# The 32x32 diagonal blocks of a triangular inverse: TensorE doubling levels, or substitution on GpSimd

## The reference

```
decay = exp(where(incl, g[..., :, None] - g[..., None, :], NEG_INF))
L = where(strict, einsum('bhnid,bhnjd->bhnij', kb, k) * decay, 0.0)
T = triangular_solve(L + eye, eye, left_side=True, lower=True)
u = einsum('bhnij,bhnje->bhnie', T, vb)
```

## Time and profile before

| What | Value |
|---|---|
| Median of 3 runs | 1326.43 us (1325.88 to 1328.53) |
| Span of the profiled execution | 1324.9 us; the page gives no other time of that execution |
| TensorE busy | 1280.8 us, 97% of the span |
| VectorE busy | 797.9 us, 60% |
| ScalarE busy | 614.3 us, 46% |
| GpSimd busy | 22.8 us, 2% |
| Mean granted TensorE clock | 0.990 of full speed |
| HBM read | 219.22 MB, 169 GB/s over the span with the writes |

### The profile page before, as it was taken

The page is one execution under the profiler, slowest core; times in us unless marked ns, Lnnn a source line. Parts: engine busy times, 40 slices in busy tenths (PEclk is TensorE's granted clock), DMA queues, the critical chain, the costliest instruction groups (busy, mean ns, idle before and its releaser), DMA issues. The chain is left out here.

```text
span 1324.9 us, 17917 instructions
## 1 busy us (share of the span) xinstructions
PE 1280.8 (97%) x7296; PEld 1110.6 (84%) x7296; DVE 797.9 (60%) x1064; ACT 614.3 (46%) x869; POOL 22.8 (2%) x36
## 2 busy tenths in 40 slices
PE   7999999999999999999999999799999999999996
PEld 6999988998998878888888888678888787878885
DVE  5668776764775455546454555567466766466553
ACT  4555545223422445543444444254445555466443
POOL 0100000000000000000000000000000000000000
PEclk9999999999999999999999999899999999999998
DMA  8646554444444454566666686455645654454662
GB/s 276 181 128 193 177 184 131 128 128 134 127 138 130 128 176 140 174 189 191 189 193 187 193 318 197 128 190 162 188 143 159 192 159 143 143 192 155 223 193 79
DMA packets 119778, 224.58 MB, mean 170 GB/s; under 512 B 9409, under 2 KB 20833, under 8 KB 118545
## 3 DMA queue, kind: packets, MB, share of 16 engines
q1 hardware_dynamic: 118386, 213.81, 52.9%
q0 software_dynamic: 1312, 9.63, 2.0%
HBM read 219.22 MB, written 4.19 MB: 169 GB/s over the span
## 5 line engine op out<-in xcount | busy, mean ns | idle before, releaser
L1076 DVE TENSOR_TENSOR lo_w<-raw_w,hi_w 128x1024 fp32r<-128x1024 f32 x396 | 479.5, 1221 | 337.2 <-ACT hi_w L740 336.3
L740 ACT ACTIVATE hi_w<-raw_w 128x1024 fp32r<-128x1024 f32 x396 | 410.2, 1055 | 287.5 <-PE acc L1645 202.7
L1645 PE MATMUL acc<-hi_w,h_hi 128*128 128x512 f32 (+1 forms) x832 | 333.3, 401 | 2.9 <-DVE h_lo L1084 2.6
L1645 PE MATMUL acc<-hi_w,h_lo 128*128 128x512 f32 (+1 forms) x832 | 322.8, 388 | 0.0
L1645 PE MATMUL acc<-lo_w,h_hi 128*128 128x512 f32 (+1 forms) x832 | 321.9, 387 | 0.0
L1645 PEld LDWEIGHTS acc<-hi_w,h_hi 128*128 128x128 f32 x832 | 157.5, 189 | 34.3 <-issue 5.0
L1636 PE MATMUL acc<-h_hi,hi_w 128*128 128x256 f32 x640 | 184.4, 288 | 1.4 <-DVE lo_w L1076 1.4
L1645 PEld LDWEIGHTS acc<-hi_w,h_lo 128*128 128x128 f32 x832 | 157.0, 189 | 33.1
L1645 PEld LDWEIGHTS acc<-lo_w,h_hi 128*128 128x128 f32 x832 | 157.6, 189 | 29.7 <-issue 0.7
L1636 PE MATMUL acc<-h_hi,lo_w 128*128 128x256 f32 x640 | 181.0, 283 | 0.0
L1636 PE MATMUL acc<-h_lo,hi_w 128*128 128x256 f32 x640 | 180.9, 283 | 0.0
(11 more groups left out here) (319 smaller groups left out, 1262.0 us busy)
## 6 DMA issues: line engine op xcount, KB each, us to landing
raw_w<-in_w_in SPq DMA_DIRECT2D x284, 512.0 KB, 3.8
raw_w<-in_w_out SPq DMA_DIRECT2D x64, 512.0 KB, 4.7
raw_w<-in_w_branch_a SPq DMA_DIRECT2D x16, 512.0 KB, 4.5
raw_w<-in_w_branch_b SPq DMA_DIRECT2D x16, 512.0 KB, 4.7
raw_w<-in_cmp_k_w SPq DMA_DIRECT2D x8, 512.0 KB, 4.3
raw_w<-in_cmp_v_w SPq DMA_DIRECT2D x8, 512.0 KB, 4.1
x_in<-in_x SPq DMA_DIRECT2D x4, 512.0 KB, 6.0
x<-in_x POOLq DMA_DIRECT2D x1, 2048.0 KB, 10.5
```

Source lines behind the costliest of these rows:

```text
L740: act.activation(hi_w[slot][:, 0:n], raw_w[no % RAW_SLOTS][:, 0:n], ACT.Copy).then_inc(*hi_ready.event(no))
L1076: dve.tensor_tensor(lo_w[slot][:, 0:n], raw_w[no % RAW_SLOTS][:, 0:n], hi_w[slot][:, 0:n].bitcast(F32), ALU.subtract).then_inc(*lo_ready.e ...
L1645: i = pe.matmul(to[:, t, 0:group.cols], x[at], w[:, k], start=first and k == 0 and m == 0, stop=last and k == n - 1 and m == 2)
```

## The change

The diagonal blocks of 32x32 of all 16 matrices (4 blocks each, 64 blocks) are no longer built by levels 2 to 5. As soon as a chain's `tri` is done, GpSimd issues four DMAs (`blocks_away`), one for each row of blocks, that write them to DRAM. When all are there, `solve` loads the 64 blocks, one to a partition with 1024 values, sets the diagonal to one, and inverts each by substitution: 31 steps of an outer product and an addition, with a wait after each instruction. It writes the result to DRAM, and eight DMAs (32 partitions, 8 heads, runs of 128 bytes) put it on the diagonal of `inv_t`, which was zeroed at the start. `lift` (VectorE) keeps the upper triangle and prepares level 6; levels 6 and 7 stay. The plan puts the first parts of all four chains in ticks 55 to 72, the solve at 73, the lifts at ticks 91, 94, 99 and 102, both quads' recurrence by tick 112. `low_t` gets a buffer for each chain, and quad 1's `gu` waits for the outgoing blocks of quad 0, whose tile it overwrites.

The plan, and the new or changed steps:

```diff
+            s = base + 4 * (NT * h + t)
             at(s, "gu", h, t)
             at(s + 1, "gram", h, t)
             at(s + 2, "decay", h, t)
             at(s + 3, "tri", h, t)
             at(s + 4, "tri_flip", h, t)
-            at(s + 5, "invert_first", h, t)
-            for n in range(2, LEVELS + 1):
-                at(s + 8 + 3 * (n - 2), "invert_y", h, t, n)
-                at(s + 9 + 3 * (n - 2), "invert_t", h, t, n)
+            at(s + 5, "blocks_away", h, t)
+    at(base + 18, "solve")
+    base += 36
+    for h in range(2):
+        for t in range(NT):
+            s = base + 8 * h + 3 * t
+            at(s, "lift", h, t)
+            for n in range(BLOCK_LEVELS + 1, LEVELS + 1):
+                at(s + 1 + 3 * (n - BLOCK_LEVELS - 1), "invert_y", h, t, n)
+                at(s + 2 + 3 * (n - BLOCK_LEVELS - 1), "invert_t", h, t, n)
                 if n < LEVELS:
-                    at(s + 10 + 3 * (n - 2), "invert_flip", h, t, n)
-        s = base + 29
+                    at(s + 3 + 3 * (n - BLOCK_LEVELS - 1), "invert_flip", h, t, n)
+        s = base + 8 * h + 9
         for n in range(5):
             at(s + n, "delta", h, n)
...
+            pool.memset(inv_t[:], 0.0).then_inc(*pool_did.event("inv_zero"))
...
+            def blocks_away(h, t):
+                pool.wait_ge(*dve_did.after("tri", h, t))
+                for b in range(4):
+                    pool.dma_start(block_scratch[0][b, t, quad(h)].rearrange("i r c -> r i c"),
+                                   diagonal_block(chain[t]["wide"], b)).then_inc(*blocks_out[h][t].event(b))
+
+            def solve():
+                for h in range(2):
+                    for t in range(NT):
+                        pool.wait_ge(*blocks_out[h][t].after(3))
+                x = small_block
+                n = x.shape[0]
+                pool.dma_start(x[:], block_scratch[0].rearrange("b t i r c -> (b t i) r c")).then_inc(
+                    *blocks_in.event(0))
+                pool.wait_ge(*blocks_in.after(0))
+                link(pool.memset(x[:].rearrange("p r c -> p (r c)")[:, 0:BLOCK * BLOCK:BLOCK + 1], 1.0))
+                for j in range(BLOCK - 1):
+                    rows, cols = j + 1, BLOCK - 1 - j
+                    term = small_term[:, 0:rows * cols].rearrange("p (r c) -> p r c", c=cols)
+                    link(pool.tensor_tensor(term, x[:, j + 1:BLOCK, j].unsqueeze(1).broadcast_to([n, rows, cols]),
+                                            x[:, 0:rows, j].unsqueeze(2).broadcast_to([n, rows, cols]), ALU.mult))
+                    to = x[:, 0:rows, j + 1:BLOCK]
+                    last = pool.tensor_tensor(to, to, term, ALU.add)
+                    if j < BLOCK - 2:
+                        link(last)
+                last.then_inc(*pool_did.event("solved"))
+                pool.wait_ge(*pool_did.after("solved"))
+                pool.dma_start(block_scratch[1].rearrange("b t i r c -> (b t i) r c"), x[:]).then_inc(
+                    *solved_out.event(0))
+                pool.wait_ge(*solved_out.after(0))
+                for b in range(4):
+                    for t in range(NT):
+                        pool.dma_start(diagonal_block(inv_t[:, :, t], b),
+                                       block_scratch[1][b, t].rearrange("i r c -> r i c")).then_inc(
+                            *blocks_back.event(b, t))
...
+                if h:
+                    dve.wait_ge(*blocks_out[0][t].after(3))
+                    dve.wait_ge(*act_did.after("tri_flip", 0, t))
                 dve.tensor_tensor(chain[t]["wide"][:], over_heads(upto[:]), over_cols(g[:, o:o + QUAD]),
                                   ALU.mult).then_inc(*dve_did.event("gu", h, t))
...
+            def lift(h, t):
+
                 inv_q = inv_t[:, quad(h), t]
-                dve.wait_ge(*act_did.after("tri_flip", h, t))
-                dve.tensor_tensor(c["inv"][:], c["wide"][:], over_heads(levels[:, 1]), ALU.mult)
-                link(dve.tensor_tensor(inv_q, c["low_t"][:], over_heads(levels[:, 2]), ALU.mult))
-                dve.tensor_tensor(c["inv"][:], c["inv"][:], over_heads(ident[:]), ALU.add)
-                dve.tensor_tensor(inv_q, inv_q, over_heads(ident[:]), ALU.add)
-                unit_columns(h, t, 2)
-                masked(h, t, 2).then_inc(*dve_did.event("masked", h, t, 2))
+                if (h, t) == (0, 0):
+                    dve.wait_ge(*blocks_back.after(3, NT - 1))
+                    for t_ in range(NT):
+                        dve.wait_ge(*act_did.after("tri_flip", 1, t_))
+                link(dve.tensor_tensor(inv_q, inv_q, over_heads(upto[:]), ALU.mult))
+                unit_columns(h, t, BLOCK_LEVELS + 1)
+                masked(h, t, BLOCK_LEVELS + 1)
+                dve.transpose(chain[t]["inv"][:], inv_q).then_inc(*dve_did.event("lift", h, t))
```

More of the change, by code:

```diff
@@ L42 @@
 BLOCK_LEVELS = 5
+BLOCK = 2 ** BLOCK_LEVELS
 RAW_SLOTS = 5
@@ L421, in build @@
         chain = [{n: arena(f"{n}{t}", [P, QUAD, P], F32, 48 + 8 * t + 2 * i)
-                  for i, n in enumerate(("low_t", "low_m", "inv", "wide"))} for t in range(NT)]
+                  for i, n in enumerate(("low_m", "inv", "wide"))} for t in range(NT)]
+        low_t = [[arena(f"low_t{h}{t}", [P, QUAD, P], F32, (54 + 8 * t, 96 + 2 * t)[h]) for t in range(NT)]
+                 for h in range(2)]
+        small_block = arena("small_block", [2 * NT * 4 * QUAD, BLOCK, BLOCK], F32, 100)
+        small_term = arena("small_term", [2 * NT * 4 * QUAD, BLOCK * BLOCK // 4], F32, 104)
         delta_u, delta_s, delta_r = (arena(f"delta_{n}", [P, QUAD, P], F32, 100 + 2 * i) for i, n in enumerate("usr"))
@@ L483, in build @@
         aux = ctx.enter_context(nc.psum_tensor("aux", [P, AUX, COLS], F32))
+        block_scratch = [nc.dram_tensor(f"{n}_scratch", [4, NT, HEADS, BLOCK, BLOCK], F32, kind="Internal").ap()
+                         for n in ("block", "solved")]
         scratch = nc.dram_tensor("x2_scratch", [SEQ, D], F32, kind="Internal").ap()
@@ L507, in build @@
         pool_did = signal("pool_did")
+        blocks_out = [[signal(f"blocks_out{h}{t}", 16) for t in range(NT)] for h in range(2)]
+        blocks_in = signal("blocks_in", 16)
+        solved_out = signal("solved_out", 16)
+        blocks_back = signal("blocks_back", 16)
         flip_source = signal("flip_source")
@@ L714, in finish @@
                 root(r3, tot, 1.0 / D, ("r3",))
-            steps = {"token_out": token_out, "delta_norm": delta_norm, "branch": branch,
+            steps = {"token_out": token_out, "delta_norm": delta_norm, "branch": branch, "blocks_away": blocks_away,
+                     "solve": solve,
                      "norm1": norm1, "norm2": norm2, "residual": residual, "att": att, "finish": finish}
@@ L840, in tri_flip @@
                 act.wait_ge(*pe_did.after("tri_flip", h, t))
-                act.activation(chain[t]["low_t"][:], aux[:, 3].rearrange("p (i c) -> p i c", c=P), ACT.Copy).then_inc(
+                act.activation(low_t[h][t][:], aux[:, 3].rearrange("p (i c) -> p i c", c=P), ACT.Copy).then_inc(
                     *act_did.event("tri_flip", h, t))
             def invert_flip(h, t, n):
-                if n <= BLOCK_LEVELS:
-                    return
                 act.wait_ge(*pe_did.after("invert_flip", h, t, n))
@@ L1221, in tri @@
                 dve.tensor_tensor(c["low_m"][:], c["inv"][:], over_heads(levels[:, 0]), ALU.mult)
-                link(dve.tensor_tensor(c["low_t"][:], c["inv"][:], over_heads(upto[:]), ALU.mult))
-                dve.tensor_tensor(attn_t[:, quad(h), t], aux[:, 2].rearrange("p (i c) -> p i c", c=P), c["low_t"][:],
+                link(dve.tensor_tensor(low_t[h][t][:], c["inv"][:], over_heads(upto[:]), ALU.mult))
+                dve.tensor_tensor(attn_t[:, quad(h), t], aux[:, 2].rearrange("p (i c) -> p i c", c=P), low_t[h][t][:],
                                   ALU.mult)
@@ L1233, in masked @@
                 c = chain[t]
-                return dve.tensor_tensor(c["low_m"][:], c["low_t"][:], over_heads(levels[:, n + 1]), ALU.mult)
+                return dve.tensor_tensor(c["low_m"][:], low_t[h][t][:], over_heads(levels[:, n + 1]), ALU.mult)
             def unit_columns(h, t, n):
@@ L1267, in invert_t @@
                     unit_columns(h, t, n + 1)
[L1269 to L1275, removed]
             def delta(h, n):
@@ L1540, in _ @@
                      "token_out": token_out, "gu": gu,
-                     "tri": tri, "invert_first": invert_first, "invert_y": invert_y, "invert_t": invert_t,
-                     "invert_flip": invert_flip, "delta": delta, "delta_norm": delta_norm, "z_out": z_out, "att": att, "flip": flip,
+                     "tri": tri, "lift": lift, "invert_y": invert_y, "invert_t": invert_t,
+                     "delta": delta, "delta_norm": delta_norm, "z_out": z_out, "att": att, "flip": flip,
```

(10 more changed lines are left out.)

8 lines of the change are left out of this document (2 added, 6 removed).

## The result

The changed kernel takes **1316.23 us** (median of four runs, 1315.72 to 1317.21) against 1326.43 before: the ratio is 0.9919, its 95% interval 0.9907 to 0.9931. It is 0.8% faster. The forecast was 1334 us and the likelier sign was slower; the time lies inside the range given, and within 1.3 us of what the second rival gave.

The account below looks back on a forecast made before the run. TensorE's own instruction order was taken to bound the kernel; −24.9 us of its work, +30.1 us standing for the blocks and +2.0 us clock gave +7.2 us, 1334 us against 1326.4, with 8 in 10 within 1305 to 1350.

Parts of the forecast that it names:

- the second rival: VectorE's splits don't shut GpSimd out of SBUF: stall 11.7 us, 1315 us; chance 0.33 with (1) and all W under 37.
- the removal: TensorE loses levels 2 to 5: 32 groups of 0.91 us, 29.1 us, and one wait of 1.4 us.
- the clock behind the stand: TensorE's granted clock drops to 1.2 GHz after standing about 30 us: +2.0 us.
- the way out and back: Blocks through DRAM after the solve: 4.9 us out, 9.1 us for all eight issues back.
- The packing: New tick order makes TensorE wait for a PSUM bank's reader at 7 places of 0.8 us: +5.6 us, bounds 2 and 10.
- W: GpSimd's own work in the 31-step solve: 17.4 us fixed plus 27.3 us for elements, 45 us; low 27, high 66.
- shut out by splits: VectorE splits of two SBUF inputs block GpSimd until they end: 15.4 splits of 1.22 us, 18.8 us during the solve.
- TensorE's own account: TensorE's saving less closer packing, if blocks are back in time: −29.1 − 1.4 + 5.6 = −24.9 us.
- (1): Solve ends by 293, blocks back at 307, stall 0: 1301.5 us; chance 0.33 with the second rival and all W under 37.
- (3): The GpSimd solve is dear, W = 66 us: stall 51 us, 1354 us; chance 0.10 together with (4) and (5).
- (4): GpSimd shuts VectorE out, splits late, some 0.5 us in each of 18 pieces: 1343 us; chance 0.10 with (3) and (5).
- (5): Quad 1's gu waits for outgoing blocks: no cost, or some 2 us at twice the issue price, 1336 us; 0.10 with (3), (4).

Follow-up runs that it names:

- late46: The changed kernel with all lifts ten ticks later (late half at 46 in place of 36), nothing else: 1298.13 us, ratio 0.9775.
- nosub36: The changed kernel without the 31 substitution steps on GpSimd, both DRAM trips and all waits kept: 1299.21 us, ratio 0.9777.
- early28: The changed kernel with all lifts eight ticks earlier (28 in place of 36): 1332.8 us, ratio 1.0032.
- merged DMAs: The changed kernel with its way back cut from eight DMAs to four, both token tiles in one: 1316.48 us, ratio 0.9912.

## Why the prediction was wrong

**Where the bound is, and that the saving is real: right.** TensorE's own order set the time before and does after; 30.5 us were counted for the removal; 31.0 were measured by the medians, 29.6 by the traces.

**Where everything stands: right.** The solve was to start at 263 and did at 263.1; VectorE was to stand in the lift from 306.3 and did from 307.7; TensorE was to wait from 312.6 and did from 313.5; the lift's four instructions were to take 2.4 us and took 2.4, from 327.54 to 329.93; the clock behind the stand was to cost 2.0 and cost 1.9. Piece times from the earlier trace rows carried over 90 us to within 1.4 us.

**The failed step is the length of TensorE's stand: 30.1 us forecast, 16.4 measured.** The mechanism was the forecast one; its terms were too dear, the solve (63.3 against 55.0) and the way out and back (14.0 against 9.5). The packing beside it was too dear as well:

| term | predicted | measured |
|---|---|---|
| fixed part of W, 62 instructions | 17.4 | 15.9 |
| elements of W, 10,912 | 27.3 (2.5 ns) | 23.7 (2.4 and 1.9 ns) |
| W | 45 | 39.2 (39.6 by the two rows above) |
| shut out by splits | 18.8 (15.4 × 1.22), 18.3 in the sum | 15.8 (16 × 0.99) |
| solve | 63.3 | 55.0 |
| out and back | 14.0 | 9.5 (318.07 to 327.54) |
| TensorE's wait | 30.1 | 16.4 |
| removal, with its wait | −30.5 | −29.6 |
| packing | +5.6 | about +2 |
| TensorE's own account | −24.9 | −27.6 |
| clock | +2.0 | +1.1 over the whole execution (1.9 of it behind the stand, 0.8 less elsewhere) |
| sum | +7.2 | −10.1 |

Of the 17.3 us between the sums, 13.7 are the wait: 8.3 from the solve, 4.5 from the way out and back, 0.9 because TensorE's work before it lasted longer. Another 2.7 are TensorE's own account, and 0.9 the clock.

The per-element rate was put at 2.5 ns from a memset's 0.92, and the fixed part at 0.28 us from one linked pair. Both were near; the sum was near a tipping point. The prediction itself put the sign's turn at W = 37.8. With W as measured, 39.2, and all else as forecast it would have said +1.4: no change, within what can be told. It was the way out and back (the DMA out landed in 2.9 us and not 4.1; the eight back were issued in 4.7 and home 6.0 after the first issue, not the 9.1 estimated from a transfer of 64-byte runs), the packing and the shutting out, some 11 us between them, that turned the sign. W, the way back and the packing had each been taken a little under the middle of its bounds (45 of 27 to 66, 9.1 of 6 to 15, 5.6 of 2 to 10), and the last two came out at the lower bound, 6.0 and about 2. Several terms leaning one way made a sign out of what was an even case.

The shutting out was right in kind and a fifth too dear for each split. The prediction let the split win every time. In the changed kernel each of the 16 splits in the solve lengthens one GpSimd instruction, but 8 of the 16 are held up themselves: they last 22.10 / 16 = 1.38 us in place of 1.22. So GpSimd loses 0.99 us a split and not 1.22, and VectorE 0.16.

**The rivals.** (1) The solve in time: not so here, but late46 and nosub36 show its price right, 1298.13 and 1299.21 us against 1301.5. (2) No shutting out, 1315: it came nearest to the time, for the wrong reason, and that the time lies in the range, which had been widened for this rival, is luck in the same way; early28, the change and late46 with 8, 16 and 21 splits and 46.75, 54.95 and 59.29 us of solve refute it. (3) and (4) fall, by the wait of 16.4 us and by nosub36. (5) The gu of quad 1 doesn't wait for the outgoing blocks: the only wait that their DMAs end is GpSimd's own, 3.15 us at 257.91, and the only wait of VectorE from 190 to 460 us that a DMA ends is the 19.9 in the lift.

Not settled by times: the packing's 2 us and the merged DMAs' 1.8 stand in the traces, of one execution each.

## What to carry to other kernels

Work that moves to an idle engine saved its full time on the busy one here (less 2 us for the closer order), once it was back before an in-order queue reached the instruction that needs it; ahead of that point it is free, behind it every microsecond counts, so look first at how many ticks lie between and move the consumer (one number here was worth 18 us). Where a forecast is a small difference between a saving and a stall, write down the value at which the sign turns and treat all terms with the same bias; several of them a little dear are a wrong sign. Count the waits that a new order takes away as well as those it adds. Before two spans are compared to 1 us, see what each lost to the clock elsewhere.

## What the runs showed of the hardware

- A two-input instruction on GpSimd over 64 partitions costs 0.16 to 0.20 us and 2.4 ns an element (a product of two broadcast columns) or 1.9 ns (an addition in place), with 0.075 us between linked ones: 0.24 us for 31 elements, 0.79 for 256. The pow rows of 1.64 and 0.71 us say nothing of it; the linked pair's 0.28 us for 8 elements does.
- SBUF is shut in both directions: a GpSimd instruction of 0.8 us takes 1.7 beside a split, a split of 1.22 takes up to 1.80 beside GpSimd (at 284.03 in the changed kernel), an extra VectorE product 1.26 in place of 0.68. A VectorE reduce with one input, 0.67 us, neither waits nor shuts out, and neither does a product of a PSUM and an SBUF tile, 1.23 us.
- After TensorE had stood for 16.4 us its granted clock was 0.50 over the next 4 us, about as after the stretch in the earlier trace rows; the price was about the same as well, 1.9 us here and 2.0 there. Of early28's span, 17.1 us above the change's, 14.2 are its longer wait, 0.8 a bank wait more and 2.4 the clock: it cost 2.8 behind the longer stand, against 2.0, and 1.7 in a stretch at 385, where the change has full clock. These make 17.4, the 17.1 to within what the traces give.
- Stretches of lower clock at other places (about 390, 1055 and 1105 us) come in some executions and not in others, and cost 1.7 us each (from windows of 1 us).
- DMAs of 128-byte runs issued by GpSimd: 0.54 to 0.59 us an issue, 1.9 us to landing for 256 runs; 0.66 an issue for 512, and 2.3 to landing.
